# Dense products behind the scans: eight half-size block products against seven, with the sums of activations on VectorE

## The chip, the cores and the metric

The kernel runs on one core of a Trainium2 chip, as one launch. The metric is the device time of one execution in microseconds (us); lower is better. Engines are named as in the profile: PE (TensorE matmuls), PEld (its weight loads), DVE (VectorE), ACT (ScalarE), POOL (GpSimd) and SP (the engine that issues most DMAs).

## The reference, cut to what matters

One layer of a hybrid backbone for 1024 latent and 128 context tokens (1152 together, `T`), width 1024 (`D`), all in float32:

```python
xn = rms_norm(x, norm1_g) * (1 + sc1) + sh1
z = xn @ w_in                      # projections, then 16 heads of RWKV-7 scans in both directions
x_a = (ln + bonuses) * g_out       # result of the scans
y_a = x_a @ w_pa
y_b = (cb * conv3(cc * ch)) @ w_pb
mix = (gate_a * y_a + gate_b * y_b) @ w_o          # gates are sigmoids
x = x + gt1 * mix
xn = rms_norm(x, norm2_g) * (1 + sc2) + sh2
x = x + gt2 * (square(relu(xn @ w_ff1)) @ w_ff2)   # w_ff1: 1024 x 4096, w_ff2: 4096 x 1024
y = rms_norm(x, final_norm_g)
```

The case is about the part from `y_b` on: the products with `w_pb`, `w_pa`, `w_o`, `w_ff1` and `w_ff2`. As products of a 1152 x 1024 with a 1024 x 1024 matrix they are eleven: one each for the first three and four each for the feed-forward weights.

## The kernel before, in words

The input projections and the scans come first, pair of heads by pair; they are the same in both kernels. Behind them all activations are held transposed, as eight planes of 128 channels (partitions) by 1152 tokens.

A float32 product is done in three float32r matmuls. Each operand is split into a high part, rounded to float32r by an ACT copy (`high`, L1559, for weights; L1604 and others for activations), and a low part, the rest, by a subtraction. The low part of weights is made on POOL (`low`, L739; two inputs from SBUF, 128x1024), that of activations on DVE (L2042, L2037, L2081, L2095; two inputs from SBUF). The matmuls are hi*hi, hi*lo and lo*hi (`wave3`), each with a 128x128 stationary block and 384 moving columns, since the tokens go in three groups of 384 (`G`, `GN`). One block of 128 output channels by 384 tokens is accumulated in one PSUM bank over 24 matmuls (12 in the second feed-forward product), then read out by DVE: gated (L2052, L2056), added to the residual (L2071, L2117), or passed through relu (L2103) and squared (L2105). Four weight buffers `ring` are filled by SP, two pairs `wsp` hold the split parts, six banks go round.

The feed-forward is taken in eight parts of 512 hidden channels (`FFE`), in a loop of which the engines run seven rounds: 12 blocks of the hidden layer, then 24 half-depth blocks of the output. Before it, the second norm stands between two products: the squares are summed over all channels, and the scaled planes are made one after another while PE waits (L2075 to L2084, L1585 to L1596).

Order on each engine is the order of its own instruction stream, and semaphores tie the streams: `o_full` counts filled banks, `o_free` emptied ones, `wh_ok` and `wl_ok` the split weights, `h_ok`, `n2_ok` and `mix_ok` the split activations. An engine whose instruction waits holds back all that is queued behind it.

Of the kernel before, what the change touches and what calls it, by code (L numbers as in the profile page):

```python
# [180 lines left out]

class Chain:
# [14 lines left out]
def flow_step(nc, xs, xp, wblocks, pack, packl, vecs, csil_in, consts, gfin, y_out, yp_out, st_out):  # L197
    ctx = ExitStack()
    with ctx:
# [23 lines left out]
        ring = [sb(ctx, f"ring{s}", [P, KT, P]) for s in range(RING)]  # L223
        wsp = [[sb(ctx, f"wsp{x}{q}", [P, KT, P], F32R) for x in range(2)] for q in range(2)]
# [54 lines left out]
        def sub_tmp(p, d, n, m):  # L279
# [59 lines left out]
        mix_hi = sb(planes, "mix_hi", [P, KT, T], F32R)
        xa_hi = sb(planes, "xa_hi", [P, KT, T], F32R)  # L340
        xn2_lo = sb(planes, "xn2_lo", [P, KT, T], F32R)
        planes.close()
        fin = ExitStack()
        xb = sb(fin, "xb", [P, KT, T])
        yof = sb(fin, "yof", [P, KT, T])
        xa = sb(fin, "xa", [P, KT, T])
        mix_lo = sb(fin, "mix_lo", [P, KT, T], F32R)
        gts = sb(fin, "gts", [P, 2, 2, T])
        xts = sb(fin, "xts", [P, 2, T])
        mtmp = sb(fin, "mtmp", [P, GN])  # L350
# [12 lines left out]
        fin.close()
# [9 lines left out]
            dve_chain pool_chain a_in b_in gt_in0 gt_in1 gt_in2 gt_in3 xh_ok xl_ok xt_in0 xt_in1 wh_ok wl_ok o_full o_free raw_ok hi_ok mix_ok sq_ok acc_ok  # L373
            sum_full rs_a2 xs_ok raw2_ok n2hi_ok n2_ok hsq_ok hhi_ok h_ok fin_full fin_sq fin_sum fin_std fin_free fin_out gf_in""".split()
# [5 lines left out]
        MIX_FILLS, WO_FILLS, FF_FILLS = 6 * KT, 3 * KT, 3 * (HB + KT)  # L380

        FF0 = MIX_FILLS + WO_FILLS
        FF_LAST = FF0 + (FFE - 1) * FF_FILLS
        OUT_LAST = FF_LAST + G * HB
        PIECES = KT // 2
        TILE_AFTER = (1, 4, 7)

        def tile_banks(t):

            if t < NC - 2:  # L390
                return banks[6:8]
            return banks[0:2] if t == NC - 2 else banks[2:4]
# [1855 lines left out]
```

## Time and profile before

| | |
|---|---|
| median of 3 runs | 2814.54 us (2813.74 to 2826.76) |
| span of the profiled execution | 2809.6 us |
| PE, PEld busy | 96%, 91% of the span |
| DVE, ACT, POOL busy | 52%, 30%, 30% |
| projections and scans, up to the first matmul with `w_pb` | 1643.6 us |
| dense products behind them | 1149.1 us |
| last tiles of the final norm | 16.9 us |

The profiled execution has no time of its own beside its span; the median of the runs is 4.9 us above the span, which lies around the first and last instruction. Shares are of the span. In the second part of the page the span is cut into 40 slices of 70 us, so the dense part is the last 16 of them.

### The profile page before, as it was taken

The page shows a single profiled execution, that of the slowest core. Times are in us where ns is not written, and L with a number is a line of the kernel's source. Part 1 is how long each engine was busy: PE and PEld are TensorE (multiplying, and loading weights), DVE is VectorE, ACT ScalarE, POOL GpSimd, SP SyncE. Part 2 cuts the span into 40 slices and gives each one's busy share as a digit, 9 for nine tenths or more (in the row PEclk, how much of TensorE's full clock was granted, in tenths as well). Part 3 has the DMA queues.
Part 4 walks back from the last instruction along what each step waited for, and adds up shares of the span by engine and source line. Part 5 has one row for each costly group of instructions (what it writes and reads, how often), then busy time and mean ns, then how long its engine had stood idle before and what let it go on. Part 6 is the DMA issues. An engine that isn't in the chain of part 4 may idle for free.

```text
span 2809.6 us, 65299 instructions
## 1 busy us (share of the span) xinstructions
PE 2697.5 (96%) x27766; PEld 2547.6 (91%) x27766; DVE 1474.7 (52%) x2774; ACT 844.6 (30%) x1547; POOL 833.3 (30%) x898
## 2 busy tenths in 40 slices
PE   4999999999999989999999989999799999999998
PEld 3899999999999977888888879998799999999997
DVE  4355585575664836876666642532633333333334
ACT  3434334244343323333333421111411111111113
POOL 1222233222222335555555522222122121121213
PEclk9999999999999989999999999999899999999999
DMA  7342533425425354445444552212111111111101
GB/s 311 102 141 72 180 88 125 144 83 161 138 69 180 90 176 127 142 133 147 134 135 136 155 203 80 88 56 75 34 45 38 45 38 44 45 37 45 45 31 68
DMA packets 276315, 293.86 MB, mean 105 GB/s; under 512 B 76128, under 2 KB 215776, under 8 KB 275936
## 3 DMA queue, kind: packets, MB, share of 16 engines
q1 hardware_dynamic: 268400, 259.26, 29.9%
q0 software_dynamic: 5904, 24.12, 2.3%
q10 hardware_dynamic: 1760, 6.82, 0.6%
q8 instruction: 196, 3.21, 0.5%
q14 instruction: 55, 0.45, 0.1%
HBM read 198.76 MB, written 91.36 MB: 103 GB/s over the span
## 4 chain that ended last, share of the span: by engine, by line
PE 93%; issue 2%; DVE 2%; DMA 1%; POOL 1%; ACT 1%; SPq 0%; DVEq 0%; POOLq 0%; ACTq 0%
PE gbank L775 26%; PE bank L775 24%; PE inv L775 23%; PE ser L775 17%; PE inv L977 1%; DMA ring<-in_wblocks 1%; PE bank L960 1%; DVE xr L1712 1%; DVE gmat L1885 0%; POOL wsp L739 0%; PE ser L1285 0%; DVE xb L2128 0%; SPq L454 0%; POOL xn_lo L665 0%; ACT xn_raw L1629 0%
## 5 line engine op out<-in xcount | busy, mean ns | idle before, releaser
L739 POOL TENSOR_TENSOR wsp<-ring,wsp 128x1024 fp32r<-128x1024 f32 x85 | 208.7, 2455 | 813.4 <-ACT wsp L1559 789.8
L659 POOL TENSOR_TENSOR wsp<-ring,wsp 128x1024 fp32r<-128x1024 f32 x67 | 205.1, 3061 | 666.3 <-ACT wsp L1347 666.3
L775 PE MATMUL gbank<-xn_hi,wsp 128*128 128x384 f32 x1312 | 348.9, 339 | 18.9 <-DVE xn_lo L2081 17.6
L775 PE MATMUL bank<-xn_hi,wsp 128*128 128x384 f32 x1312 | 346.6, 338 | 2.9 <-issue 2.5
L775 PE MATMUL inv<-xn_hi,wsp 128*128 128x384 f32 x1312 | 343.4, 337 | 0.8 <-issue 0.8
L775 PEld LDWEIGHTS gbank<-xn_hi,wsp 128*128 128x128 f32 x1312 | 240.7, 189 | 23.2 <-issue 16.0
L775 PEld LDWEIGHTS bank<-xn_hi,wsp 128*128 128x128 f32 x1312 | 239.8, 189 | 2.6 <-POOL wsp L739 0.7
L775 PEld LDWEIGHTS inv<-xn_hi,wsp 128*128 128x128 f32 x1312 | 238.1, 188 | 1.8 <-POOL wsp L659 1.1
L775 PE MATMUL ser<-xn_hi,wsp 128*128 128x384 f32 x816 | 218.5, 341 | 6.0 <-POOL xn_lo L665 6.0
L1559 ACT ACTIVATE wsp<-ring 128x1024 fp32r<-128x1024 f32 x85 | 89.5, 1053 | 443.6 <-PE inv L775 364.5
L775 PE MATMUL gbank<-xn_lo,wsp 128*128 128x384 f32 x656 | 221.9, 338 | 0.0
L775 PE MATMUL bank<-xn_lo,wsp 128*128 128x384 f32 x656 | 221.5, 338 | 0.0
L775 PE MATMUL inv<-xn_lo,wsp 128*128 128x384 f32 x656 | 220.5, 336 | 0.0
L1885 DVE TENSOR_TENSOR gmat<-gbank,gmask 128x1024 f32<-128x1024 f32 x144 | 175.6, 1220 | 49.5 <-PE gbank L775 48.7
L775 PE MATMUL gbank<-ub 64*64 64x128 f32 (+1 forms) x3456 | 182.4, 315 | 7.4 <-DVE gmat L1885 6.7
L775 PE MATMUL bank<-mix_lo,wsp 128*128 128x384 f32 x832 | 160.2, 335 | 1.0 <-POOL wsp L769 1.0
L775 PE MATMUL gbank<-mix_lo,wsp 128*128 128x384 f32 x832 | 160.8, 336 | 0.0
L775 PE MATMUL inv<-mix_lo,wsp 128*128 128x384 f32 x832 | 160.1, 335 | 0.0
L775 PEld LDWEIGHTS ser<-xn_hi,wsp 128*128 128x128 f32 x816 | 150.0, 189 | 8.9 <-POOL xn_lo L665 7.1
L1604 ACT ACTIVATE mix_lo<-gts 128x384 fp32r<-128x384 f32 x96 | 50.5, 526 | 323.2 <-DVE gts L2105 323.2
L775 PEld LDWEIGHTS bank<-mix_lo,wsp 128*128 128x128 f32 x832 | 145.6, 188 | 1.4 <-POOL wsp L769 1.4
L775 PEld LDWEIGHTS gbank<-mix_lo,wsp 128*128 128x128 f32 x832 | 146.0, 188 | 0.0
(397 smaller groups left out, 5504.9 us busy)
## 6 DMA issues: line engine op xcount, KB each, us to landing
ring<-in_wblocks SPq DMA_DIRECT2D x195, 512.0 KB, 4.1
ub<-op_d SPq DMA_DIRECT2D x144, 256.0 KB, 2.8
op_d<-ar SPq DMA_DIRECT2D x32, 576.0 KB, 5.4
op_d<-bk SPq DMA_DIRECT2D x32, 576.0 KB, 6.2
vb<-v_d SPq DMA_DIRECT2D x144, 64.0 KB, 3.1
xt_d<-xt_s POOLq DMA_DIRECT2D x8, 576.0 KB, 6.8
x_d<-zero SPq DMA_DIRECT2D x8, 576.0 KB, 6.8
v_d<-vn SPq DMA_DIRECT2D x8, 576.0 KB, 6.8
```

The costliest lines, as they stand in the source:

```text
L659: GT(wsp[s % 2][1][:], ring[(N_ADA_RING + s) % RING][:], wsp[s % 2][0][:].bitcast(F32), ALU.subtract).then_inc(S["wsplit_lo"], 1)
L739: nc.gpsimd.tensor_tensor(wsp[b % 2][1][:], ring[(N_MIX0 + b) % RING][:], wsp[b % 2][0][:].bitcast(F32), ALU.subtract).then_inc(S["wl_ok"], 1)
L775: return nc.tensor.matmul(out, lhsT, rhs, start=start, stop=stop)
L960: ins = nc.tensor.transpose(banks[3][:, y * P:(y + 1) * P], ub[v % LOADS][:, y // 2, 2 + y % 2, :], ident[:])
L977: ins = nc.tensor.transpose(inv[:, 0, x * P:(x + 1) * P], xt[:, place_of(v), :, :].rearrange("p h t -> p (h t)"), ident[:])
L1559: A(wsp[b % 2][0][:], ring[slot][:], ACT.Copy).then_inc(S["wh_ok"], 1)
L1604: A(hid_hi[:, s, cols(cg)], hsq[:, (G * s + cg) % 2, :], ACT.Copy).then_inc(S["hhi_ok"], 1)
L1712: ins = V.tensor_scalar(xr[:, c % 2, a:b], banks[1 + n % TURNS][:, a - cg * GN:b - cg * GN], mul1[:, c, kind:kind + 1], mods[:, c, kind:ki ...
L1885: V.tensor_tensor(gmat[v % SETS][:, d, :, :, :].rearrange("p h x t -> p h (x t)"), gbank[:, :, :], gmask[:, d:d + 1, :].to_broadcast([P, 2 ...
```

## The change

The diff replaces everything behind the scans. Tokens are halved (`TH` = 576), and so are the channels of both operands (`KH` = 4 blocks of 128), so that each of the eleven 1024-wide products becomes a 2x2 block product. It is done as seven block products (numbers 2, 1, 6, 5, 3, 7, 4, in that order) of sums and differences of the quadrants, in place of eight plain ones. A block product is 8 groups (4 blocks of output channels by 2 quarters of tokens of 288 columns) of 4 x 3 matmuls: 96 matmuls with 288 moving columns. Some of the seven are accumulated on what the bank still holds (`OPENS` names those that begin anew).

Sums of weights (`w_sum_out`, 128x512, for products 2, 6, 5, 7, 4) are made on POOL, one ahead of the low part (`w_low`). Sums of activations (`a_parts`, 128x576: 8 operations for product 6, 4 for 5, 12 for 3, 4 for 7) and all low parts of activations (`a_low`, 4 for each product) are made on DVE. Results are read from the banks group by group by ACT (products 2, 6, 5 of the first two and the `w_ff1` products, and product 3 of `w_ff1`) or DVE (all others), added to or copied into the quadrant they belong to, and finished there (`finish`: gate, or relu and square, 128x576). The second norm is spread over the products of `w_o` and of the first `w_ff1`. Gates and the residual are loaded by SP in place of POOL, and weights by quadrants into `raw_w`. All loops are written out. In the diff `group` is PE's, `w_sum_out` and `w_low` are POOL's, `w_high` is ACT's (a weight buffer is free when PE is through with it), and the rest is DVE's.

```diff
+ORDER = (2, 1, 6, 5, 3, 7, 4)
+DENSE = ["pb", "pa", "wo"] + ["f1", "f2"] * 4
+PRODUCTS = len(ORDER) * len(DENSE)
...
+            def group(q, g):
+                (m, th), n = divmod(g, 2), KH * q
+                op = product_of(q)[1]
+                if q:
+                    read_out(q - 1, g)
+                pe.wait_ge(S["wl_ok"], n + m + 1)
+                hi, lo = w_hi[(n + m) % 4], w_lo[(n + m) % 4]
...
+                for k in range(KH):
+                    if g == 0:
+                        pe.wait_ge(S["al_ok"], n + k + 1)
+                    s = (n + k) % (2 * KH)
+                    chain(o, hi[:, k, :], a_hi[s][:, to], op in OPENS and k == 0, False)
+                    chain(o, hi[:, k, :], a_lo[s][:, to], False, False)
+                    ins = chain(o, lo[:, k, :], a_hi[s][:, to], False, k == KH - 1)
+                ins.then_inc(S["o_full"], 1)
...
+            w_sum_out(0)
+            for n in range(KH * PRODUCTS):
+                if n + 1 < KH * PRODUCTS:
+                    w_sum_out(n + 1)
+                w_low(n)
...
+            def w_high(n):
+                (q, m), s = divmod(n, KH), n % 4
...
+                if q:
+                    act.wait_ge(S["o_full"], 2 * KH * (q - 1) + 2 * m + 2)
...
+            def a_parts(q):
...
+                if op in SUMMED_A:
+                    dve.wait_ge(S["o_full"], 2 * KH * (q - 1))
...
+                for k in range(KH):
+                    o = a_sum[(KH * q + k) % (2 * KH)][:]
+                    if op == 6:
...
+                        ch.step(V.tensor_tensor(o, plane(x, "21", k), plane(x, "22", k), add))
...
+                for k in range(KH):
+                    a_low(q, k)
...
+            for q in range(PRODUCTS - 1):
...
+                a_parts(q + 1)
...
+                    read_out(q)
```

On POOL, before, the end of the product with `w_o` and the start of the feed-forward loop (`wsp` are the split weights, `ring` the raw ones, `gts` here the gain of the final norm):

```order
L757 DMA xts<-xt_d 128x1152 [waits o_free]
L739 TENSOR_TENSOR wsp<-ring,wsp 128x1024 [waits wh_ok] x2
L760 DMA gts<-in_gfin 128x1024 [waits sum_full]
L761 UNCONDITIONAL_BRANCH
L761 ISA
L739 TENSOR_TENSOR wsp<-ring,wsp 128x1024 [waits wh_ok]
L738 REGISTER_ALU
```

and POOL of the changed kernel, in the last `w_ff2` product, where the weights of products 6, 5 and 3 are made (`raw_w` raw, `w_sum` and `zsum` summed):

```order
L927 TENSOR_TENSOR zsum<-zsum,raw_w 128x512 [waits ws_ok]
L946 TENSOR_TENSOR w_lo<-zsum,w_hi 128x512 [waits wh_ok]
L931 TENSOR_TENSOR w_sum<-raw_w 128x512 [waits o_full]
L946 TENSOR_TENSOR w_lo<-zsum,w_hi 128x512 [waits wh_ok]
L931 TENSOR_TENSOR w_sum<-raw_w 128x512 [waits o_full]
L946 TENSOR_TENSOR w_lo<-w_sum,w_hi 128x512 [waits wh_ok]
```

Before, POOL's stream in the feed-forward holds one subtraction for 128x1024 weights and nothing else. Now a sum stands ahead of nearly every subtraction, and most sums wait for PE to be through with the buffer (`o_full`).

On DVE, before, the hidden layer in the last round of the feed-forward (`gts` holds relu and square, `mix_lo` the split hidden layer):

```order
L2110 COMPARE_AND_BRANCH
L2103 TENSOR_SCALAR gts<-gbank 128x384 [waits o_full]
L2105 TENSOR_TENSOR gts<-gts 128x384 [waits o_free]
L2103 TENSOR_SCALAR gts<-gbank 128x384 [waits o_full]
L2105 TENSOR_TENSOR gts<-gts 128x384 [waits o_free]
L2095 TENSOR_TENSOR mix_lo<-gts,mix_lo 128x384 [waits hhi_ok]
L2103 TENSOR_SCALAR gts<-bank 128x384 [waits h_ok,o_full]
```

and DVE of the changed kernel in a `w_ff1` product, from the parts of product 6 to those of 7 (`r` are the activations and results, `a_sum` and `a_lo` the sums and low parts):

```order
L2273 TENSOR_TENSOR a_sum<-r 128x576 [waits n2_ok] x3
L2290 TENSOR_TENSOR a_sum<-a_sum,r 128x576 [waits dve_chain] x4
L2259 TENSOR_TENSOR a_lo<-a_sum,a_hi 128x576 [waits ah_ok] x4
L2299 TENSOR_TENSOR r<-gbank,r 128x288 [waits o_full] x2
L2299 TENSOR_TENSOR r<-bank,r 128x288 [waits o_full] x2
L2328 SCALAR_TENSOR_TENSOR r<-r 128x576 [waits read_d]
L2299 TENSOR_TENSOR r<-inv,r 128x288 [waits o_full] x2
L2328 SCALAR_TENSOR_TENSOR r<-r 128x576 [waits read_d]
L2299 TENSOR_TENSOR r<-ser,r 128x288 [waits o_full] x2
L2328 SCALAR_TENSOR_TENSOR r<-r 128x576 [waits read_d] x2
L2276 TENSOR_TENSOR a_sum<-r 128x576 [waits o_full]
```

Before, relu, square and low part of one 384-column piece followed the bank that they read. Now the parts of the next product (here 12 operations of product 6) stand ahead of the results of the current one (here product 1), and the parts of the product after follow.

## Rows read from the trace of the kernel before

**Rows 1.** Page, parts 1 and 2: busy us, and granted clock in 40 slices.
```profile
PE 2697.5 (96%) x27766; PEld 2547.6 (91%) x27766; DVE 1474.7 (52%) x2774; ACT 844.6 (30%) x1547; POOL 833.3 (30%) x898
...
PEclk9999999999999989999999999999899999999999
```

**Rows 2.** Busy time by stretch: busy us (instructions) of each engine, clock, DMA.
```profile
core 0: us, PE busy (x) PEld busy (x) DVE busy (x) ACT busy (x) POOL busy (x), PEclk, DMA share, GB/s
...
1643.60:2792.70 1149.10, 1120.08 (x6385) 1114.70 (x6386) 435.03 (x732) 209.80 (x287) 249.25 (x128) 0.99 0.17 58
1852.00:1862.00 10.00, 7.60 (x36) 7.61 (x37) 3.53 (x6) 1.47 (x2) 2.37 (x1) 0.83 0.16 52
1950.00:1995.00 45.00, 24.64 (x105) 21.26 (x104) 29.82 (x20) 24.44 (x29) 0.57 (x1) 0.77 0.08 24
```

**Rows 3.** Waits of PE from 1636 us on: us in total, times, longest us.
```profile
PE gbank L775 <- DVE xn_lo L2081: 17.6, 6, 13.8
PE gbank L775 <- POOL wsp L739: 11.0, 1, 11.0
...
PE gbank L775 <- DVE mix_lo L2037: 2.7, 1, 2.7
```

**Rows 4.** Chain that ended last: start us, us, matmuls in a row.
```profile
1766.92 8.48 PE inv L775 x48
...
1864.33 8.38 PE bank L775 x48
...
2086.66 8.32 PE gbank L775 x48
```

**Rows 5.** Groups by shape: count, busy us, mean ns of one, idle before.
```profile
L2117 DVE SCALAR_TENSOR_TENSOR x<-bank,mods,x 128x384 f32<-128x384 f32 x28 | 17.3, 618 | 37.4 <-PE bank L775 37.4
L2117 DVE SCALAR_TENSOR_TENSOR x<-bank,mods,x 128x128 f32<-128x128 f32 x28 | 9.6, 342 | 0.0
L2052 DVE SCALAR_TENSOR_TENSOR mix_raw<-gts,bank 128x384 f32<-128x384 f32 x8 | 4.4, 555 | 25.7 <-PE bank L775 25.7
L2058 DVE TENSOR_TENSOR mix_raw<-mix_raw,mtmp 128x384 f32<-128x384 f32 x24 | 13.4, 558 | 0.8
L2042 DVE TENSOR_TENSOR xa_lo<-xa,xa_hi 128x1152 fp32r<-128x1152 f32 x8 | 10.2, 1353 | 0.7 <-ACT xa_hi L1572 0.7
L739 POOL TENSOR_TENSOR wsp<-ring,wsp 128x1024 fp32r<-128x1024 f32 x80 | 195.5, 2444 | 763.7 <-ACT wsp L1559 763.7
L703 POOL TENSOR_TENSOR xtb<-xt,trim 128x128 f32<-128x128 f32 x22 | 9.5, 431 | 47.4 <-DVE tt L1879 19.0 <-DVE xt L1902 18.6 <-issue 9.8
L1596 ACT ACTIVATE xn_hi<-xn_raw 128x1152 fp32r<-128x1152 f32 x8 | 9.3, 1168 | 0.3
L1604 ACT ACTIVATE mix_lo<-gts 128x384 fp32r<-128x384 f32 x96 | 50.5, 526 | 323.2 <-DVE gts L2105 323.2
```

**Rows 6.** DVE in order of time at 248 us: start us, us, instruction.
```profile
247.00 1.36 DVE L1761 TENSOR_TENSOR ar<-ar,mid 128x1152 f32<-128x1152 f32 x1
248.39 3.52 DVE L1763 TENSOR_TENSOR ar<-ar 128x1152 f32<-128x1152 f32 x1
251.83 3.83 DVE L1768 TENSOR_TENSOR kd<-kd,kt 128x1152 f32<-128x1152 f32 x1
255.59 0.48 DVE L1798 CAST vn<-eye 72x256 f32<-72x256 bf16 x2
```

**Rows 7.** POOL in the same stretch.
```profile
248.28 2.41 POOL L659 TENSOR_TENSOR wsp<-ring,wsp 128x1024 fp32r<-128x1024 f32 x1 [14.65 <-ACT wsp L1347]
250.65 3.81 POOL L671 TENSOR_TENSOR kd_r<-kd,cv_r 128x1152 fp32r<-128x1152 f32 x1
```

**Rows 8.** The end of the span, in order of time.
```profile
2803.09 1.41 DVE L2128 SCALAR_TENSOR_TENSOR xb<-gbank,frs,gts 128x512 f32<-128x512 f32 x2
...
2805.12 1.41 DVE L2128 SCALAR_TENSOR_TENSOR xb<-bank,frs,gts 128x512 f32<-128x512 f32 x2
2806.56 0.33 SPq L643 DMA_DIRECT2D yp_out<-xb  x1
```

More of the change, by code:

```diff
@@ L339, in flow_step @@
[L339 to L350, printed above, removed]
@@ L363, in flow_step @@
-        fin.close()
+        post = ExitStack()
+        r1, r2 = (sb(post, n, [P, KT, T]) for n in ("r1", "r2"))
+        zsum = sb(post, "zsum", [P, KH, HW])
+        w_hi = [sb(post, f"w_hi{s}", [P, KH, P], F32R) for s in range(4)]
+        w_lo = [sb(post, f"w_lo{s}", [P, KH, P], F32R) for s in range(4)]
+        a_hi = [sb(post, f"a_hi{s}", [P, TH], F32R) for s in range(2 * KH)]
+        a_lo = [sb(post, f"a_lo{s}", [P, TH], F32R) for s in range(2 * KH)]
+        r3 = sb(post, "r3", [P, KT, T])
@@ L1598, in _ @@
-            n_ff = MIX_FILLS + WO_FILLS
-            def hidden(it, s):
-                for cg in range(G):
-                    act.wait_ge(S["hsq_ok"], G * HB * it + (G * s + cg + 1))
-                    A(hid_hi[:, s, cols(cg)], hsq[:, (G * s + cg) % 2, :], ACT.Copy).then_inc(S["hhi_ok"], 1)
-            def feed_forward(it, last):
-                for b in range(2 * HB):
-                    used = n_ff + (G * b if b <= HB else G * HB + 2 * G * (b - HB))
-                    if not (last and b == 2 * HB - 1):
-                        high(2 * N_BRANCH + KT + b + 1, it, 2 * HB, FF_FILLS * it + used)
-                    if b < HB:
-                        hidden(it, b)
@@ L1625, in final_root @@
+            for q in range(PRODUCTS - 1):
+                period(q)
             def final_root(t):
@@ new lines, in gained_out @@
+            def gained_out(q, g):
+                (u, op), (m, th) = product_of(q), divmod(g, 2)
+                quad = QUAD_OF[op]
+                at, h = place_q[quad]
+                gain = hgt1[:, at + m, :] if DENSE[u] == "wo" else mods[:, 40 + at + m, :]
+                if DENSE[u] == "wo":
+                    dve.wait_ge(S["x2_in"], 16 * X_ORDER.index(quad) + 16)
+                dve.wait_ge(S["o_full"], filled_at(q, g))
+                x = part(r2, quad, m, th)
+                edge = LAT - TH - GH
+                for a, b, kind in ((0, edge, 0), (edge, GH, 1)) if h and th else ((0, GH, 0),):
+                    ins = stt(x[:, a:b], banks[g][:, a:b], gain[:, kind:kind + 1], x[:, a:b], mul, add)
+                ins.then_inc(S["read_d"], 1)
@@ new lines, in read_out @@
+            def read_out(q, some=range(2 * KH)):
+                u, op = product_of(q)
+                kind = DENSE[u]
+                if kind in ("wo", "f2"):
+                    for g in some:
+                        gained_out(q, g)
+                elif reader(q) == "D":
+                    for g in some:
+                        if op == 3:
+                            gated_out(q, g)
+                        else:
+                            add_out(q, g)
+                        if g % 2 and g > 1:
+                            finish(q, g // 2 - 1)
+                    finish(q, KH - 1)
```

838 lines of the change are left out of this document (504 added, 334 removed).

## The prediction, made blind

> **What bounds the kernel now.** I read the page's busy shares first, then the busy time by stretch, PE's waits, and the chain that ended last. PE is busy 96% of the span at full clock in nearly all slices [rows 1]: it is the bound, and a change pays by what it takes off PE. The change touches only the stretch from 1643.6 to 2792.7 us, 1149.1 us, in which DVE is busy 435 us and POOL 249 [rows 2]. The two long waits in it are the start (11.0 us for the first split weights) and the second norm (17.6 us for `xn_lo`, the longest 13.8) [rows 3]. Around the norm the clock is 0.77 [rows 2]; together with two waits of near 3 us the stretch loses about 49 us beside its matmuls: these are 3 x 576 + 2 x 2304 = 6336, and 48 of them take 8.32 to 8.48 us [rows 4], 173.3 to 176.7 ns each, so 1100 us.
>
> **PE after the change.** 11 x 7 = 77 block products of 96 matmuls are 7392, with 288 columns in place of 384. No such matmul is in the trace. If only the 96 columns fall away, at 2.4 GHz (40 ns), one costs 133.3 ns; in proportion to columns 130.0; without anything beside its columns 120; without any gain from fewer columns 173.3. I take 131, near the proportional end, since the step varies with the operand (8.32, 8.38, 8.48), as something that streams would. That is 968 us, 12.58 us for a block product, against 1100: 132 us less, and 181 less than the whole stretch if PE never waited. At 133.3 it would be 17 us more.
>
> The Trainium skill (TensorE: Matmul & The Clock Gate, "Back-to-back issue gap") gives columns over 2.4 GHz plus 2.5 ns when warm. The row disagrees: 173.3 ns for 384 columns, where the rule makes 162.5. By the rule the 7392 would take 905 us.
>
> **The other engines' prices.** On DVE two inputs from SBUF cost 558 ns for 384 elements and 1353 for 1152 [rows 5], so 0.75 us for 576. A read of PSUM by the gain is 618 at 384 and 342 at 128, so 0.52 at 288; a plain one is 555 at 384, so 0.45 [rows 5]. Where a quarter of the tokens crosses from latent to context it is cut in two (160 and 128 columns, 0.72), half the reads of four of the seven products. On POOL 128x1024 takes 2444 ns and 128x128 431 [rows 5]: 512 take 1.27. ACT's copies of 576 are about 0.7 (526 and 1168 for 384 and 1152 [rows 5]), of 512 0.65; per product 4 + 4 + up to 8 reads of 0.4 are near 9 of 12.6 us, so ACT is no bound.
>
> **What POOL and DVE do to each other.** At 248.39 a DVE operation with two SBUF inputs, 1.36 us alone, takes 3.52, and the next 3.83 [rows 6]; POOL's 2.41 us one began just before, and POOL's next takes 3.81 in place of some 2.67 (2444 x 1152/1024, less its fixed part) [rows 7]. They take turns. The steps between DVE's starts, 3.44 and 3.76 us, are POOL's 2.2 ns an element plus DVE's 1.04. So a turn of the new shapes holds POOL's path for 1.13 us (512) and DVE's for 0.60 (576); reads of PSUM stay outside. Now count: POOL does 77 x 4 = 308 low parts and 11 x 5 x 4 = 220 sums, 528; DVE 308 low parts, 308 additions for sums, about 90 finishing steps and 30 for the norm, some 735. The shared path is held 528 x 1.13 + 735 x 0.60 = 1038 us, more than PE's 968. It cannot all hide.
>
> The Trainium skill (SBUF — State Buffer, on the shared port pair) says more: an exclusive lock, held for the whole instruction, and it counts DVE operations with two SBUF inputs among those that take it. That the two exclude each other the rows show; that whole durations add they don't quite: 3.44 and 3.76 against 3.77 and 4.03. By the rule the path is held 528 x 1.27 + 735 x 0.75 = 1222 us, and the stretch would be longer than today's 1149.
>
> **One unit of seven products, by hand.** DVE's stream is: parts of the next product, then results of this one. Next product's first group needs its parts and the first read, so it starts about 0.5 us after the parts end. The parts can't begin before PE is through with the product before (plus 0.7 us for its last read, where DVE reads). POOL offers about two operations (sum, low) in each 3.15 us of PE, and 3 to 4 of them fall on DVE's parts, each a 1.13 us block; those under PSUM reads cost nothing. Products whose parts fit take PE's 12.6 us.
> - `w_ff1` unit: products 2, 3, 7, 4 take 12.6 each, 50.3. Parts of 6: 12 x 0.75 + 4 x 1.13 = 13.5, so 14.2. Parts of 5 wait behind the reads and four finishing steps of product 1 (8 x 0.45 + 4 x 0.75 + 1.1 = 7.7): 7.2 + 6 + 4.0 + 0.5 = 17.7. Parts of 3: 16 x 0.75 + 3 x 1.13, 15.5. Sum 97.7.
> - `w_ff2` unit (DVE reads all): 2, 7, 4 at 12.6, 37.7. Before 6: 14.7. Before 5: reads 3.6, then 6 + 4.5 + 0.5, 14.6. Before 3: 16.2. Before 7: reads 4.4, then 11, 15.4. Sum 98.6.
> - `w_o` as `w_ff2`, 98.6; `w_pb` 99; `w_pa` with 16 additions more, 107.
>
> Together 391 + 394 + 305 = 1090 us. The norm is spread over four products: 30 DVE operations (22 us) and 32 on ACT, partly hidden, and two round trips for which PE waits: 15 us; what I don't see is whether it costs 5 or 35. The clock: behind a wait of 2.7 us [rows 3] the stretch 1852 to 1862 shows 0.83 [rows 2], a part of it at 1.2 GHz, 1.7 us lost. Waits of 2 to 5 us now come three or four to a unit; if one in seven brings such a fall, that is 10 us. Stretch: 1090 + 15 + 10 = 1115, 14.5 us for a product against the break-even of 1149 / 77 = 14.9.
>
> Moved or free: gate, residual and weight loads go to SP. The DMA share is 0.17 in the stretch [rows 2] and each quadrant is asked for about a unit ahead; cover is a product's 12.6 us against some 4 to 7 us of transfer, without it 5 us a unit. The start still needs a split weight block first: 0 to -3 us. The end stays: the last tiles follow each other by 2.03 us, and five of them after the last group [rows 8] need about what now stands in the last 16.9 us; plus or minus 3. The scans are not touched.
>
> **Sum.** 1643.6 + 1115 + 16.9 = 2775.5 for the span, against 2809.6; with the 4.9 us by which the median lies above the span, **2780 us**, 1.2% faster. The likeliest case's own range is 2745 to 2815.
>
> **Rivals.**
> - A: PE stays the bound. POOL's work falls under DVE's PSUM reads and idle time, and lag is made up in the light products (2, 4, 7). For it: alone, DVE needs 51 + 11 us in a `w_ff1` unit and 42 + 32 in a `w_ff2` unit, and POOL 48 x 1.27 = 61, all under PE's 88. Against it: the shared path's 1038. 1643.6 + 968 + 15 + 17 + 5 = 2649; half of my waits saved, 2715.
> - B: lockstep. If DVE's parts meet nearly all of POOL's work, a `w_ff1` unit is DVE's 51 + 11 reads + 48 x 1.13 - 48 x 0.15 of fixed parts hidden = 109, a `w_ff2` unit 42 + 32 + 47 = 121. PE stalls delay POOL's wake-ups into the next parts, which feeds it. Midway between this and my 98 the units average 107: 1180 + 25 makes a stretch of 1205 and a time of **2870**, slower; it decides from a mean of 104.5 us a unit on. The skill's rule lands there too: 1643.6 + 1222 + 17 + 5 = 2888. Against it: 2.41 + 1.36 is not what the rows add up to.
> - C: a matmul costs 173.3 ns whatever its columns: 7392 make 1281 us and 2946 us. Against it: with the same 128x128 weights the step still differs with the operand (8.32, 8.38, 8.48 [rows 4]), so columns, not weight loads, seem to pace it.
> - That the change doesn't remove matmul work is excluded by the count.
>
> **Chances.** My case 0.52, A 0.20, B 0.25, C 0.03. Within 0.5% (2800 to 2829), about what a measurement of this kernel can't tell from no change, lie 0.12 of my case and 0.02 of B. Faster: 0.40 + 0.20 = 0.60; same 0.14; slower 0.23 + 0.03 = 0.26. The range takes in half of A and most of B: 2675 to 2885.
>
> **What the profile will show.** Step of a 288-column matmul 130 to 134 ns (C: 173). In the feed-forward, PE waits at the first groups of products 6, 5 and 3 of a unit, 2 to 5 us each, for `a_lo` or the reads on DVE; products 2 and 4 without waits. DVE's 128x576 operations average near 1.1 us in place of 0.75, POOL's near 1.4. DVE busy 80% or more of the stretch. If they average 0.8, A holds; if units take over 104.5 us, B. The prediction fails if the waits fall on ACT or POOL's `w_lo` chain, or if the clock stays below 0.95 over the stretch.

## The result, and the profile after

The changed kernel takes 2838.23 us (median of 6 runs, 2834.12 to 2843.08) against 2815.18 (2813.62 to 2830.64) of the kernel before, run beside it: ratio 1.0066, 95% interval 1.0044 to 1.0089. It is slower by 0.66%, 23 us, where 2780 us and faster had been forecast. The profiled execution's span is 2836.3 us, so the median lies 1.9 us above it.

The page of the changed kernel, busy us (share) of each engine [rows 1 of before]:

```profile
PE 2616.7 (92%) x28864; PEld 2462.9 (87%) x28864; DVE 2031.5 (72%) x3316; ACT 1100.9 (39%) x2132; POOL 1453.9 (51%) x1297
...
PE   4999999999999989999999978787789999899898
...
DVE  4355584575655836876667678897879979888797
ACT  3434334244343413333333334324543443443434
POOL 1322223232321335555545468775587788687784
PEclk9999999999999999999999999898899999999999
```

PE fell from 96% to 92%, and from slice 24 on DVE stands at 7 to 9 tenths and POOL at 4 to 8. The stretches [rows 2]: the whole changed one from the first product to the last block, one `w_ff1` unit, one `w_ff2` unit, and the units with the norm (`w_o` and the first `w_ff1`).

```profile
core 0: us, PE busy (x) PEld busy (x) DVE busy (x) ACT busy (x) POOL busy (x), PEclk, DMA share, GB/s
1649.10:2818.80 1169.70, 1040.54 (x7472) 1031.66 (x7473) 1001.16 (x1262) 465.46 (x861) 871.91 (x525) 0.94 0.15 53
...
2412.10:2514.10 102.00, 93.10 (x675) 92.70 (x673) 81.45 (x88) 46.35 (x92) 78.31 (x48) 0.95 0.12 42
2514.10:2613.70 99.60, 92.88 (x674) 92.21 (x673) 92.56 (x134) 34.34 (x56) 78.98 (x50) 0.97 0.13 43
...
1869.50:2110.80 241.30, 200.64 (x1392) 198.02 (x1393) 200.76 (x258) 102.89 (x187) 153.22 (x92) 0.89 0.12 41
```

1149.1 us became 1169.7. DVE's work in it went from 435 to 1001 us, POOL's from 249 to 872. The waits of PE from 1640 us on [rows 3]:

```profile
PE gbank L1399 <- POOL w_lo L946: 67.4, 9, 14.2
PE gbank L1399 <- DVE r L2355: 29.7, 13, 2.8
PE ser L958 <- DVE r L2382: 19.4, 2, 10.3
PE gbank L1399 <- ACT r L1751: 12.1, 5, 2.8
PE gbank L1399 <- DVE r L2299: 9.0, 1, 9.0
```

The largest part of the standing time, 67.4 of 142 us, ends with POOL's low parts of the weights (L946), the rest with reads of the banks on DVE and ACT and with the norm's additions (L2382). Groups by shape from 1650 to 2740 us: count, busy us, mean ns of one, idle before [rows 5]:

```profile
L2259 DVE TENSOR_TENSOR a_lo<-r,a_hi 128x576 fp32r<-128x576 f32 x123 | 198.9, 1673 | 62.1 <-ACT a_hi L1722 62.0
L2259 DVE TENSOR_TENSOR a_lo<-a_sum,a_hi 128x576 fp32r<-128x576 f32 x162 | 150.8, 984 | 21.8 <-ACT a_hi L1722 21.8
...
L2290 DVE TENSOR_TENSOR a_sum<-a_sum,r 128x576 f32<-128x576 f32 x84 | 57.8, 745 | 0.0
```

An operation of 576 elements takes 745 ns on average in one group and 1673 in another, and 1.18 us over all 729 of them. POOL's 524 operations of 512 elements average 1.69 us. Four groups of 12 matmuls each, in 3.18 us twice over:

```profile
2412.30 3.18 PE gbank L1399 x24
2415.48 3.18 PE bank L1399 x24
```

That is 132.5 ns a matmul (the mean step at full clock is 133.1, over 6973 of them).

**Where the time went.** From the starts of the 7392 matmuls: 7392 x 133.0 = 983.1 us; 373 of them, behind waits, follow each other by 241.8 instead, 40.6 us more; PE stands 145.5 us in 45 gaps. Sum 1169.2 of 1169.7. In the same terms the forecast had 968, 10 and 137.

**The lock-out.** DVE and POOL in unit `pa`, in order of time: start us, us, instruction; what ended the idle time before.

```profile
1792.01 2.76 DVE L2276 TENSOR_TENSOR a_sum<-r 128x576 f32<-128x576 f32 x4
1794.69 2.75 DVE L2259 TENSOR_TENSOR a_lo<-a_sum,a_hi 128x576 fp32r<-128x576 f32 x4
1797.36 2.75 DVE L2278 TENSOR_TENSOR a_sum<-r 128x576 f32<-128x576 f32 x4
1800.04 2.75 DVE L2285 TENSOR_TENSOR a_sum<-a_sum,r 128x576 f32<-128x576 f32 x4
1802.71 2.75 DVE L2290 TENSOR_TENSOR a_sum<-a_sum,r 128x576 f32<-128x576 f32 x4
```

```profile
1787.11 1.80 POOL L946 TENSOR_TENSOR w_lo<-zsum,w_hi 128x512 fp32r<-128x512 f32 x1
1788.87 1.82 POOL L931 TENSOR_TENSOR w_sum<-raw_w 128x512 f32<-128x512 f32 x1
1796.78 9.80 POOL L946 TENSOR_TENSOR w_lo<-w_sum,w_hi 128x512 fp32r<-128x512 f32 x1 [6.10 <-ACT w_hi L1741]
1806.55 1.29 POOL L931 TENSOR_TENSOR w_sum<-raw_w 128x512 f32<-128x512 f32 x1
```

While DVE issues without a break (20 operations, 0.67 us apart, none lengthened), POOL's operation, which alone takes 1.29, begins at 1796.78, beside the last `a_lo`, and ends at 1806.59, 1.1 us after the run has ended (1805.47). PE stands from 1792.2 to 1806.7, at the first group of product 5, and goes on when it is through. Not all of these 14.5 us is the lock-out: up to 1796.78 POOL itself waits for ACT's `w_hi`, and 8.5 us are what the operation took too long. The same happens in `pb` and in each `w_ff1` unit before product 3, with a `w_lo` of 4.47 us. Up to 1790.7, where POOL was there first, the two take turns and each operation takes 1.8. Of POOL's 524 operations from 1649 us on 276 took 1.7 to 2.0 us, and 27 took more than 2.0.

`pa` has a second long wait, 9.0 us for DVE (L2299 above), before the first group of `w_o`. From 1855.7 to 1869.0 us DVE goes through four finishing operations and four low parts ahead of that read, and seven of the eight are in turns with POOL, at about 1.8 us each. In e1, below, this wait is gone.

### The profile page after: what moved, and what is told of

It reads as the page before. It is cut to its first block, busy times and chain, and to the rows that moved or that the text cites. A ratio compares the mean times of both kernels' runs of the same rounds, so it can differ in the third digit from the quotient of the medians.

```text
span 2836.3 us, 68929 instructions
## 1 busy us (share of the span) xinstructions
PE 2616.7 (92%) x28864; PEld 2462.9 (87%) x28864; DVE 2031.5 (72%) x3316; ACT 1100.9 (39%) x2132; POOL 1453.9 (51%) x1297
## 4 chain that ended last, share of the span: by engine, by line
PE 69%; DVE 18%; POOL 5%; issue 3%; ACT 2%; DMA 2%; SPq 1%; DVEq 0%; ACTq 0%; POOLq 0%
PE ser L958 17%; PE gbank L958 12%; PE bank L958 11%; PE inv L958 11%; PE gbank L1399 6%; DVE a_lo L2259 5%; PE inv L1399 4%; PE ser L1399 3%; PE bank L1399 3%; POOL w_lo L946 3%; DVE a_sum L2276 2%; POOL w_sum L931 2%; DVE a_sum L2278 2%; DVE r L2328 1%; DVE r L2299 1%
## 5 line engine op out<-in xcount | busy, mean ns | idle before, releaser
L841 POOL TENSOR_TENSOR wsp<-ring,wsp 128x1024 fp32r<-128x1024 f32 x67 | 210.6, 3143 | 671.3 <-ACT wsp L1501 671.3
L1399 PE MATMUL gbank<-a_hi,w_hi 128*128 128x288 f32 x616 | 201.3, 327 | 118.8 <-POOL w_lo L946 67.4
L946 POOL TENSOR_TENSOR w_lo<-raw_w,w_hi 128x512 fp32r<-128x512 f32 x132 | 229.2, 1750 | 135.2 <-ACT w_hi L1741 135.2
L2259 DVE TENSOR_TENSOR a_lo<-r,a_hi 128x576 fp32r<-128x576 f32 x132 | 213.8, 1676 | 66.2 <-ACT a_hi L1722 66.1
L946 POOL TENSOR_TENSOR w_lo<-w_sum,w_hi 128x512 fp32r<-128x512 f32 x132 | 214.0, 1624 | 23.1 <-ACT w_hi L1741 22.5
L1722 ACT ACTIVATE a_hi<-a_sum 128x576 fp32r<-128x576 f32 x176 | 118.4, 688 | 205.7 <-DVE a_sum L2290 133.3
L1399 PE MATMUL gbank<-a_lo,w_hi 128*128 128x288 f32 x616 | 197.5, 321 | 0.0
L1399 PE MATMUL gbank<-a_hi,w_lo 128*128 128x288 f32 x616 | 197.2, 320 | 0.0
L958 PE MATMUL gbank<-ub 64*64 64x128 f32 (+1 forms) x3456 | 179.4, 310 | 10.6 <-DVE gmat L2096 5.6
L1399 PE MATMUL inv<-a_hi,w_hi 128*128 128x288 f32 x616 | 184.2, 299 | 0.4
L1399 PE MATMUL inv<-a_hi,w_lo 128*128 128x288 f32 x616 | 183.7, 298 | 0.0
L1399 PE MATMUL inv<-a_lo,w_hi 128*128 128x288 f32 x616 | 183.5, 298 | 0.0
```

The lines of the kernel that those rows point to most:

```text
L841: GT(wsp[s % 2][1][:], ring[(N_ADA_RING + s) % RING][:], wsp[s % 2][0][:].bitcast(F32), ALU.subtract).then_inc(S["wsplit_lo"], 1)
L946: GT(w_lo[n % 4][:], w_source(n), w_hi[n % 4][:].bitcast(F32), ALU.subtract).then_inc(S["wl_ok"], 1)
L958: return nc.tensor.matmul(out, lhsT, rhs, start=start, stop=stop)
L1399: return nc.tensor.matmul(out, lhsT, rhs, start=start, stop=stop, skip_group_check=True)
L1722: A(a_hi[s][:], src, ACT.Copy).then_inc(S["ah_ok"], 1)
L2259: V.tensor_tensor(a_lo[s][:], src, a_hi[s][:].bitcast(F32), sub).then_inc(S["al_ok"], 1)
```

## The experiments

All times are medians; the ratio is to the kernel before on the same chip, with its 95% interval. Units and waits are read from the one profiled execution of each kernel. The changed kernel's is 1.0066. "Unit" is the time from the first group of one `w_ff1` or `w_ff2` unit to that of the next: 101.9 and 99.6 us in the changed kernel, 89.0 if PE never waits.

### e1: GpSimd's operations read nothing

```
-                    ins = GT(out, a[:, m, :], b[:, m, :], ALU.subtract)
+                    ins = nc.gpsimd.memset(out, 0.25)
...
-                GT(w_lo[n % 4][:], w_source(n), w_hi[n % 4][:].bitcast(F32), ALU.subtract).then_inc(...)
+                nc.gpsimd.memset(w_lo[n % 4][:].bitcast(F32), 0.0).then_inc(S["wl_ok"], 1)
```

> Every GpSimd instruction of the dense stretch (low parts of the weights, sums of the weights) is replaced by one that writes a constant to the same place and reads nothing; order, waits and semaphores stay. The low parts and the sums of the weights are thus left out of what is computed. Theory T1 (VectorE's and GpSimd's two-input operations hold one path to SBUF in turns, and GpSimd is shut out while VectorE runs back to back): VectorE's 128x576 operations fall from 1.1 us on average to 0.75 everywhere, the waits of PE in the feed-forward units all but vanish, a w_ff1 unit goes from 101.9 to 90-91 us and a w_ff2 unit from 99.6 to 90-92; with pb, pa, w_o 15-25 us less together, the time falls by 85 to 110 us, to 2728-2753. Theory T2 (the waits come from the order of the queues and the chain ACT sum -> high -> low -> PE, whatever the path): the units keep most of their waits, the time falls by less than 40 us, from GpSimd's shorter instructions alone.

2678.52 us, ratio 0.9499 (0.9463 to 0.9535): 160 us less than the changed kernel. A `w_ff1` and a `w_ff2` unit:

```profile
2297.00:2386.10 89.10, 89.10 (x675) 89.10 (x674) 54.72 (x91) 46.82 (x92) 24.00 (x48) 1.00 0.14 48
2386.10:2475.10 89.00, 89.00 (x673) 89.00 (x673) 66.74 (x129) 34.51 (x56) 23.99 (x48) 1.00 0.14 48
```

PE is busy all the time, at full clock, with the same order and the same waits in the queues. DVE does the same work in 54.7 us in place of 81.5; its 576-element operations average 752 to 758 ns in every group. The order of the queues (T2) is not the cause. But T1's forecast missed by far: 85 to 110 us were expected. `pb`, `pa` and `w_o` were to give 15 to 25 us together and gave 57 (103.7 to 91.4, 116.8 to 89.0, 116.5 to 99.6), the first `w_ff1` unit 18 (124.8 to 106.4). What e1 does not separate: POOL's instructions are shorter too (0.53 us). e7 and e14 do: in e7 VectorE takes over POOL's reading operations, in e14 POOL gets more of them.

### e2: the norm's work ahead of the parts

```
+                if q == 19:
+                    norm_adds(0, range(KH, KT))
                 a_parts(q + 1)
...
-                if q == 19:
-                    norm_adds(0, range(KH, KT))
```

and on ACT the squares of the second half ahead of `a_high` of product 22.

> The norm's four additions for the first half of the tokens go ahead of the parts of product 20 on VectorE, and its four squares for the second half go ahead of the high parts of product 22 on ACT; nothing else moves. Theory N1 (PE's two waits of 9.0 and 10.3 us in the norm come from the norm's work queued behind parts that are not needed for another product): the two waits shrink to 0-3 us each, the low clock behind them goes, 16 to 24 us less, 2814-2822. Rival N2 (the norm's own chain of squares and additions is what is late, whatever stands ahead of it): the waits stay over 7 us each or turn up at the next product's first group; within 5 us of 2838.

2832.22 us, ratio 1.0048 (1.0025 to 1.0071). Its interval overlaps the changed kernel's; the trace shows the two waits at 12.1 us together in place of 19.4:

```profile
PE ser L958 <- DVE r L2382: 12.1, 2, 9.2
```

The first went from 9.3 to 3.2 us, the second only from 10.6 to 9.5; `w_o` and the first `w_ff1` unit take 233.4 us in place of 241.3. N1 holds for the first wait, N2 for the second; the 16 to 24 us that N1 had forecast didn't come.

### e3: sums made one product earlier

In the last three `w_ff1` units, in `a_parts`, with `sum_of` the free quadrant `r1[:, KH + k, 0:TH]`:

```
+                if not is_ahead(q):
+                    a_sums_of(q)
                 for k in range(KH):
                     a_low(q, k)
+                if q + 1 < PRODUCTS and is_ahead(q + 1):
+                    dve.wait_ge(S["al_ok"], KH * q + KH)
+                    a_sums_of(q + 1)
```

> In the last three w_ff1 units the sums of activations for products 6, 5 and 3 are made one product earlier, into the quadrant of r1 that is free then; the number of operations is the same. If VectorE's lateness at 5 and 3 sets the waits and its idle time in product 2 can be used: a w_ff1 unit goes from 101.9 to 92-96 us, 18 to 30 us less in all. If the shared path is full or GpSimd is shut out by longer unbroken runs of VectorE (16 operations, 10.7 us): the units stay at 98 us or more, or grow, -10 to +20 us, and a low part on GpSimd takes up to 11 us.

2835.31 us, ratio 1.0041 (1.0016 to 1.0065), and the units take 101.8 us, as before. PE's gaps of 3.0 us before product 5 and 6.4 before product 3 became 4.4 before product 6 and 4.4 before product 3. Using DVE's idle time wins nothing: the rival held in the time and in the units. That the resource is full is not shown by this run alone: the wait of 4.4 us that now stands before product 6 could also come from where the sums stand, as it does in e10 and e15 below. (The `w_lo` of up to 11 us that the rival expected didn't come; the `w_sum` and `w_lo` around took 1.8 each.)

### e4: the weights' high part first on ACT

```
+                early = more and product_of(q + 1)[1] in (6, 5, 3)
+                if early:
+                    w_high(n)
                 for k in range(KH):
```

> The changed kernel with one reordering on ACT: for products 6, 5 and 3 the high part of the first block of weights goes ahead of the four high parts of activations in its queue, so that GpSimd can make its low part earlier. If PE's wait of 3.0 us before product 5 and part of the 6.4 us before product 3 is ACT's order (w_hi queued behind a_hi that waits for VectorE's sums; the path only second): 8 to 25 us less, w_ff1 units of 97-100 us. If VectorE's lateness, through the path, is what ends these waits: the same parts are late, w_ff1 units stay within 1 us of 101.9 or grow, since the high parts of activations now wait for PE's second group: 2834-2850.

2846.98 us, ratio 1.0092 (1.0066 to 1.0117): not faster, if anything slower. The waits move from the first group to the second and third. The lock-out comes there; in the whole stretch five low parts took 8.6 to 11.1 us each. Here two `w_lo` take 7.96 us, of which PE's third group waits 3.7:

```profile
2484.90 7.96 POOL L946 TENSOR_TENSOR w_lo<-raw_w,w_hi 128x512 fp32r<-128x512 f32 x2 [7.62 <-ACT w_hi L1741]
```

### e5: DVE pauses for GpSimd

```
                 if op in SUMMED_A:
+                    dve.wait_ge(S["wl_ok"], KH * (q - 1) + 1)
                     dve.wait_ge(S["o_full"], 2 * KH * (q - 1))
```

> One wait more on VectorE: before the sums of activations for product q it waits until GpSimd has made the first low part of the weights of product q-1. Theory S (an unbroken run of VectorE operations shuts GpSimd out; the w_lo of 4.47 us in pb and the four w_ff1 units and of 9.80 us in pa are that, and PE waits for them): those six take 2-3 us, PE's wait of 14.5 us in pa falls to 5-7, those of 6.4-7.2 us to 4-5; 15 to 28 us less with the clock's part, 2810-2823. Rival (PE would have waited anyway for VectorE's low parts, or the delayed sums come back as waits at the next product): 2833-2846.

2824.07 us, ratio 1.0017 (0.9995 to 1.0039), 14 us less than the changed kernel, by a wait that was added. The same place in `pa`:

```profile
1800.13 1.78 POOL L946 TENSOR_TENSOR w_lo<-w_sum,w_hi 128x512 fp32r<-128x512 f32 x1 [6.10 <-ACT w_hi L1741]
```

```profile
1801.95 7.14 DVE L2279 TENSOR_TENSOR a_sum<-r 128x576 f32<-128x576 f32 x4 [1.16 <-POOL w_lo L946]
```

9.80 us became 1.78, PE's wait 6.5 in place of 14.5 (those before product 3: 3.8 for 6.4; `w_ff1` units 98.7). Theory S is shown by these rows, though the 14 us lie just short of the 15 to 28 expected: the wait in `pa` fell by 8.0 us, but the unit only from 116.8 to 112.6. And DVE's next four operations take 7.14 us in place of 2.75, now that POOL is in: the lock-out is only the sharpest form of the same limit.

### e6: sums of weights on VectorE

`w_sum_out` goes to DVE, on top of e5:

```
                         gained_out(q, g)
+                        if g % 2 and q + 1 < PRODUCTS:
+                            w_sum_out(KH * (q + 1) + g // 2)
```

> With the wait of e5, and the 220 sums of weights moved from GpSimd to VectorE, each behind the reads of the block of the product before; GpSimd keeps the 308 low parts. Theory T1 (what counts is how long the shared path is held; GpSimd holds it 1.2 us for 512 elements, VectorE 0.6 to 0.7 us): although VectorE, the busiest engine beside PE, gets 220 operations more, the path is held some 100 us less; a w_ff1 unit goes from 98.7 to 93-97 us, a w_ff2 unit from 99.6 to 94-98, the time from 2824 to 2765-2795. Rival T2 (VectorE's own queue is the bound, and it is held up behind sums that wait for PE's groups): units of 99 us or more, 2820-2860.

2793.59 us, ratio 0.9903 (0.9874 to 0.9933). The last three `w_ff1` units take 95.5 to 97.1 us, the `w_ff2` units between them 96.1 and 97.2 (from an execution of 2785.1 us, the fastest of the six). The busier engine took 220 operations more, and the kernel became 1.1% faster than e5.

### e7: low parts too, GpSimd idle

```
+                V.tensor_tensor(w_lo[n % 4][:], w_source(n), w_hi[n % 4][:].bitcast(F32), sub).then_inc(S["wl_ok"], 1)
```

each one block behind the sums of e6, without e5's wait.

> Sums and low parts of the weights all on VectorE, GpSimd idle in the dense stretch. Theory T1: nothing takes turns any more; VectorE alone needs some 86 us in a w_ff1 unit (68 x 0.67 + 48 x 0.62 + 28 reads x 0.37) and 94 in a w_ff2 unit, PE 89: units of 89-92 and 94-98 us, 2740-2780. Rival T2 (VectorE's queue: every operation more on it makes the parts later, and the low parts add waits for ACT): units over 100 us, 2840-2900.

2772.48 us, ratio 0.9837 (0.9804 to 0.9871). A `w_ff1` and a `w_ff2` unit:

```profile
2361.30:2454.60 93.30, 89.75 (x674) 89.14 (x673) 82.63 (x138) 46.07 (x92) 0.00 (x0) 1.00 0.14 46
2454.60:2554.30 99.70, 92.44 (x675) 91.82 (x674) 94.97 (x179) 34.80 (x56) 0.00 (x0) 0.97 0.13 43
```

DVE does its own work and all of POOL's in 82.6 us of a `w_ff1` unit; in the changed kernel it took 81.5 for its own alone. T1 held; the units came 1 to 2 us above what it expected. Now the `w_ff2` units (98.4 to 99.7) are near what DVE itself needs (95 of 99.7).

### e8: a mixture

Low parts on DVE in `pb` and `w_ff1`, on POOL elsewhere (`continue` in POOL's loop for those units), with e5's wait.

> As e6, with the low parts of the weights on VectorE in the pb and w_ff1 units and on GpSimd in the others. Theory T1: w_ff1 units as in e7 (89-92 us), w_ff2 units as in e6 (94-98), 2745-2785. Rival T2: w_ff1 units longer than in e6.

2776.48 us, ratio 0.9843 (0.9808 to 0.9878), no different from e7: `w_ff1` 93.3, where T1 had 89 to 92, `w_ff2` 97.9. In e6 the same code took 96.1 to 99.2 us in the first three `w_ff2` units; why it varies isn't explained.

### e9: PE kept busy in the waits

```
+                filler = {5: 10, 3: 24}.get(op, 0) if g == 0 and DENSE[q // len(ORDER)] == "f1" else 0
+                for _ in range(filler):
+                    mm(banks[0][:, GH:GH + P], ident[:], ident[:], True, True)
```

What bank 0 held for the first group of products 5 and 3 is lost by it, so this kernel's time alone is used.

> Only PE's stream changes: in the w_ff1 units it runs 10 small matmuls into unused columns of a bank before product 5 and 24 before product 3, in the 3.0 and 6.4 us in which it would stand still. Theory C (the low clock behind each wait costs 3.3 us a w_ff1 unit because PE stood still): the steps at half clock behind these waits go, the waits themselves stay as long; 10-14 us less in four units, 2824-2830. Rival: the clock falls all the same, or the fillers delay the groups: 2836-2846.

2830.22 us, ratio 1.0026 (1.0008 to 1.0045). The stretch with both waits, first the changed kernel, then e9:

```profile
2450.00:2480.00 30.00, 21.10 (x131) 20.70 (x130) 26.62 (x27) 14.75 (x35) 18.82 (x10) 0.83 0.10 36
```

```profile
2451.00:2480.00 29.00, 26.96 (x207) 25.94 (x206) 27.81 (x29) 15.35 (x35) 19.59 (x10) 1.00 0.11 37
```

The clock stays at its full level, and a unit takes 99.9 us for 101.9 (8 us in the four units; the ratios differ by 0.4%, 11 us, with an uncertainty that covers both). Of the 3.5 us of slow steps in a unit 2.0 come back: product 3's 14.9 us became 12.8, but product 5's period (20.6) stayed, since the next wait ends when DVE and POOL are through, however fast PE got there.

### e10: one sum in place of three

On e7, for `w_o`, `w_ff1` and `w_ff2`: x11 + x12 - x21 - x22 is x12 minus product 6's sum.

```
+                if op == 6 and early3(u):
+                    for k in range(KH):
+                        dve.wait_ge(S["as_ok"], a_sums(q, k))
+                        V.tensor_tensor(r1[:, KH + k, 0:TH], plane(x, "12", k), a_sum[(KH * q + k) % (2 * KH)][:], sub).then_inc(S["as_ok"], 1)
```

> As e7 (all weight work on VectorE), and in the w_o, w_ff1 and w_ff2 units the sum for product 3 is made as x12 - (x21 + x22 - x11) from product 6's, into the quadrant that is free or read for the last time: 4 operations in place of 12 a unit, and they stand with product 6's. Theory T1/load (once GpSimd is out of the way, the time VectorE's stream takes beside PE's 89 us sets the unit): w_ff1 from 93.3 to 89-91 us, w_ff2 from 98.5 to 93-96, together 22 to 38 us less than e7: 2735-2752. Rival (not the load but the position counts: product 6 now has 16 operations before its first group, so it starts later by what 3 gains): within 8 us of e7, 2764-2782.

2750.16 us, ratio 0.9758 (0.9734 to 0.9783). `w_ff2` 94.1 us, as expected of the load; `w_ff1` 94.1, against 93.3 in e7, as expected of the position: a gap of 3.3 us before product 6 took the place of those at 5 and 3. Each theory held in one kind of unit: the load in `w_ff2`, the position in `w_ff1`.

### e11 and e12: the norm again

e11 is e10 with e2's edit.

> As e10, with the norm's additions and squares ahead of the parts, as in e2. There this gave 5 us; if the waits in the norm are the norm's own chain and VectorE's queue before it, 4 to 10 us less than e10; if the norm's waits just reappear at the next product, no difference (within 3 us).

2747.87 us, ratio 0.9752 (0.9727 to 0.9777). The time doesn't tell it from e10 (2750.16, 0.9758); the `w_o` unit is 2.4 us shorter. The 4 to 10 us of the first theory didn't come.

e12 moves the norm's round trip for the first half of the tokens to later groups. The spread then overwrites what groups 6 and 7 of product 19 left in their banks for product 20, so its time alone is used:

```
+                    if (q, g) in ((19, 5), (21, 3)):
+                        norm_sums((q - 19) // 2)
+                    if (q, g) in ((20, 1), (21, 5)):
+                        norm_spread(q - 20)
```

> As e11, with the first half's norm spread later over PE's stream: its sums behind group 5 of product 19 in place of group 3, its spread behind group 1 of product 20. If PE's wait of about 7 us in product 19 is for squares and additions that are simply not there yet after 3 groups: the wait falls by 3 us and the round trip is hidden, 4 to 9 us less than e11. Rival: scaling for product 21 becomes late by as much, no gain or up to 6 us more.

2746.63 us, ratio 0.9751: the same as e11. Product 19 takes 20.1 us in place of 23.5, and product 20 17.6 in place of 13.9. The rival held: a wait moved by one product.

### e13: one sum in place of three, GpSimd kept

e5 with e10's edit.

> As e5 (GpSimd keeps all the weight work), with product 3's sum made from product 6's in w_o, w_ff1 and w_ff2 units: 4 operations in place of 12 on VectorE. If a VectorE operation costs its 0.67 us there, alone or in a turn: 8 x 0.67 = 5.4 us a unit less at the most, w_ff units of 93-97 us, 2785-2805. If with GpSimd in turns the shared path is what is full, a removed VectorE operation takes only its 0.6 us from it and GpSimd's 48 x 1.2 stay: units of 95-99 us, 2795-2815. If position counts (product 6 gets 16 operations ahead of it, up to 1.8 us each in turns), 2815-2840.

2814.82 us, ratio 0.9986 (0.9964 to 1.0007), 0.3% less than e5, with intervals that just overlap. `w_ff1` 96.2 (98.7 in e5), `w_ff2` 98.4 (99.6): 2.5 and 1.2 us, where DVE's 8 operations alone would be 5.4. (The units are from an execution of 2800.4 us, one of the fastest of the twelve.) That fits a shared path which GpSimd's work still fills, but doesn't prove it: in `w_o` and in each of the eight units behind it one `w_lo` now takes 5.2 us, where the longest in e5's `w_ff1` units took 2.5, so a new lock-out may have taken a part of the gain.

### e14: one part of the change taken back

The four additions for product 5 of each unit are POOL's again, ahead of its work for that product:

```
+                    GT(a_sum[(KH * q + k) % (2 * KH)][:], plane(x, "21", k), plane(x, "22", k), ALU.add).then_inc(S["as_ok"], 1)
```

> The changed kernel with one part of the change taken back: the 4 additions for product 5's activations in each unit are GpSimd's again. Theory T1 (the path): GpSimd holds the path about twice as long for the same elements (1.35 us in place of 0.67), 0.6 x 44 = 27 us more on it, and they are queued before low parts of weights that PE waits for: the same or slower, 2835-2870. Theory T2 (VectorE's queue is too long, GpSimd stands idle for a fifth of the time): 2 to 3 us less in each of 11 units, 2805-2815.

2874.98 us, ratio 1.0203 (1.0171 to 1.0235): 1.4% slower than the changed kernel, 5 us above the range that T1 gave. DVE has 44 operations fewer, and `w_ff1` units take 105.6 us, `w_ff2` units 102.7. POOL's four take 7.09 us:

```profile
2462.15 7.09 POOL L957 TENSOR_TENSOR a_sum<-r 128x576 f32<-128x576 f32 x4
```

That product 5's sums stand on VectorE is a good part of the change, not what made it slower.

### e15: the kept sum

e11, with product 6's sum kept in the free quadrant of `r1` in `w_ff1`:

```
+                if op == 3 and kept6(u):
+                    dve.wait_ge(S["al_ok"], KH * number(u, 6) + KH)
+                    for k in range(KH):
+                        o = r1[:, KH + k, 0:TH]
+                        V.tensor_tensor(o, plane(x, "12", k), o, sub).then_inc(S["as_ok"], 1)
```

> As e11, but in the w_ff1 units product 6's sum is kept in the free quadrant and product 3's made from it just before product 3: the same 4 operations, moved from ahead of product 6 to ahead of product 3. If e10's w_ff1 units (94.1 us against 93.3 in e7) stand still before product 6 for those 4 operations: the wait of 3.3 us there shrinks to 1 or less, units of 89.5-92 us, 2730-2740. If not, 2744-2752.

**2740.25 us, ratio 0.9727 (0.9697 to 0.9757)**, the best of all: 2.7% faster than the kernel before, 3.4% faster than the changed one. A `w_ff1` unit, a `w_ff2` unit and the whole stretch:

```profile
2346.60:2438.00 91.40, 89.45 (x673) 89.04 (x673) 77.26 (x130) 46.38 (x92) 0.00 (x0) 1.00 0.14 47
2438.00:2532.00 94.00, 89.55 (x675) 89.14 (x674) 89.57 (x171) 34.64 (x56) 0.00 (x0) 1.00 0.14 46
1649.70:2721.00 1071.30, 1013.02 (x7472) 1006.79 (x7473) 960.47 (x1713) 467.58 (x861) 0.00 (x0) 0.98 0.17 59
```

The gap before product 6 fell below 0.8 us, as expected. 88 us above the 983 of its matmuls are left: 2.4 to 5 us in most units, 46 in `w_o` and the first `w_ff1` unit with the norm, 10 in `pa`.

## Why the prediction was wrong

**Its sign hung on 34 us.** The break-even was 104.5 us a unit; the forecast 101.4 (1115 / 11); measured 106.3 (1169.7 / 11). The mechanism was named rightly: DVE and POOL hold one path, it "cannot all hide", and e1, e7 and e14 show it. Rival B was this mechanism with a mean of 107 us a unit and 2870 us, and the kernel came out between the two, beyond the break-even. Point by point:

- **Matmul: mis-sized.** 131 taken, 133.1 measured: the first of the four bounds, the 96 columns alone (133.3), was right. The text priced that at 17 us; it cost 15. The reason for 131, that a step which varies with its operand streams in proportion, was not borne out. C is out.
- **The other engines' prices: right.** 0.75 for 576 elements on DVE (0.745 to 0.758 wherever POOL is out of the way), reads 0.44 and 0.52, POOL 1.27 to 1.29.
- **Turns: right in size.** Predicted 1.13 + 0.60 = 1.73 us a pair; measured 1.80. The shared path's rule of the Trainium skill (SBUF — State Buffer, "Who interferes with whom"), whole durations, would make an estimated 1.29 + 0.75 = 2.04; the traces show 1.80.
- **"3 to 4 of them fall on DVE's parts, each a 1.13 us block": right in number, wrong in kind.** 303 of POOL's 524 operations took 1.7 us or more, 3.9 a product. But turns are the case where POOL got in. Against a DVE that issues without a break it doesn't get in at all (9.80 and 4.47 us), and PE waits for the `w_lo`, not for DVE. That was a sign that I had named as failure ("waits fall on POOL's `w_lo` chain"): 67.4 us of them. e5, which lets POOL in, puts this at 14 us of the time. The same section of the Trainium skill says that the one that comes second fully blocks, and speaks of one instruction; the rows show a block over a run of 13, and the prediction had weighed the rule only by single ones.
- **One unit by hand: the sum near, the parts not.** `w_ff1` 97.7 forecast, 101.9 measured, of which 3.5 is clock and 1.3 the matmul's price; the gaps are 9.2 us against 9.6 (97.7 - 7 x 12.58). `w_ff2` 98.6 and 99.6, the gaps 7.2 against 10.5. Inside the unit the places were off: product 6 began on time, 5 was 3.0 late (5.1 forecast) and 3 was 6.4 late (2.9). `pb` 99 and 103.7; `pa` 107 and 116.8: the wait with the lock-out (14.5 us, of which 8.5 are the lock-out) and the 9.0 us wait behind DVE's turns, neither of which the working had.
- **The clock: the term that failed most, 10 forecast, 40.6 measured.** "One in seven" waits of 2 to 5 us was to bring a fall. By the granted clock in the trace, 11 of the 18 gaps of 2.4 to 3.6 us were followed by 3.4 us at 1.2 GHz, and all ten above 4 us came with 6.8 to 17.1 us of it, which began inside the gap. The granted clock over the stretch is 0.94, under the 0.95 that I had set as a sign of failure. e9 shows that it hangs on the standing still, and that only part of it (2.0 of 3.5 us a unit) is on the path that sets the end.
- **The norm: 15 forecast, about 40 measured** (241.3 us for the two units in place of 201.5), above my 5 to 35. Two waits of 9.3 and 10.6 us for its additions and one of 4.3 us before product 6 of the first `w_ff1` are in it. e2 takes 8 us off, e1 still has 28 (206.0 against 178.0): by that it is mostly a chain of its own, round trips between four engines with PE in the middle, and of it no run here says what remains if all queues were free.
- **The start: 0 to -3 forecast, +5.5 measured.** The first product began at 1649.1. In the fifteen other runs, none of which changes the scans, it began between 1642.9 and 1655.4, and 1643.6 is from the one trace of the kernel before: no run tells whether any of the 5.5 us is the change's.
- **The end:** 16.9 forecast, 17.5 measured.
- **What the profile was to show.** The matmul (130 to 134 ns), DVE's busy share (86% where 80% or more was forecast) and DVE's mean (1.18 us for near 1.1) came. POOL's mean is 1.69 us, not 1.4. In `w_ff2` units PE waits also before product 1, 2.5 us.

Sum: 15 (matmul) + 31 (clock) + 9 (standing, the norm's excess against gaps smaller elsewhere) + 5.5 + 0.6 = 61, which is 2836.3 - 2775.5.

The stretch came out 54.7 us above its forecast, and the sign needed 34. No term of the sum alone reaches that; the clock comes nearest with 31. As bookkeeping of where the time went this is complete; as a cause the clock is worth less than its 31, since in e9 only 2.0 of 3.5 us came back. All three of price, clock and norm could miss far more upwards than downwards, and I took values near the low end for each.

## What to carry to other kernels

When two engines share a path, add the time for which each holds it, and give the work to the engine that holds it for less, though it be the busier one: here 528 operations moved from an engine at half load to one at 72% took 2.3% off. A change that brings the bounding engine near a second one turns its slack into gaps of a few microseconds, and each such gap has to be priced with the low clock behind it. And look in the trace for an instruction that takes several times its usual time beside a neighbour that runs without a break: a pause for it may be worth more than the work it delays.

## What the runs showed of the hardware

- A POOL operation with two SBUF inputs, begun 0.08 us after one of DVE's in an unbroken run, lasted until the whole run was over, 12 operations more: 9.80 us for 1.29, while DVE's kept their 0.75. Where POOL was in first, the two took turns of 1.80 us a pair.
- A memset of 128x512 on POOL takes 0.53 us and doesn't lengthen DVE's operations beside it.
- The step of a matmul with 128x128 weights was 173.3 ns for 384 columns [rows 4] and 133.1 for 288: 40.2 ns for 96 columns, which is 2.4 GHz, and 13 ns left over in both shapes. The Trainium skill (TensorE: Matmul & The Clock Gate, "Back-to-back issue gap") has 2.5 ns left over, but for a matmul by itself; in a stream with weight loads, as here, it says that both set the spacing. So the prediction held its 173.3 against a rule for another case.
